# Turning the shifted bias tiles round: eight float32 matmuls with a flip matrix become 32 TensorE transposes with the same matrix

## What is computed

```python
def t5_bucket(dist):
    dist = jnp.maximum(dist, 0)
    ...
    return jnp.where(dist < BUCKET_MAX_EXACT, dist, large)
...
        bias = jnp.transpose(bias_tab[t5_bucket(dist)], (0, 3, 1, 2))
        logits = jnp.einsum('bqhd,bqkd->bhqk', qb, kg).astype(jnp.float32) * scale + bias.astype(jnp.float32)
```

## Time and profile before

| | us |
|---|---|
| median of 3 runs | 679.97 |
| lowest, highest | 677.24, 688.75 |
| the profiled execution | 680.09 |
| its span, first to last instruction | 678.3 |
| TensorE matmuls busy in the span | 614.6 |
| VectorE, ScalarE, GpSimd busy | 389.5, 309.0, 229.7 |

### The profile page before, as it was taken

The page is one execution under the profiler, slowest core; times in us unless marked ns, Lnnn a source line. Parts: engine busy times, 40 slices in busy tenths (PEclk is TensorE's granted clock), DMA queues, the critical chain, the costliest instruction groups (busy, mean ns, idle before and its releaser), DMA issues.

```text
span 678.3 us, 9664 instructions
## 1 busy us (share of the span) xinstructions
PE 614.6 (91%) x3658; PEld 389.0 (57%) x3658; DVE 389.5 (57%) x823; ACT 309.0 (46%) x502; POOL 229.7 (34%) x165
## 2 busy tenths in 40 slices
PE   1799999599899999789999999989999999799998
PEld 1344557365434866467767667755666677433443
DVE  6722394153579998986887866632325444567411
ACT  2555543223456685640431522354576676353610
POOL 1355540441203565440343341143632221143420
PEclk9999999699999999999999999998999999999999
DMA  8334533344101441320031021121121101252311
GB/s 279 93 103 138 166 104 92 125 125 124 48 1 50 124 125 31 94 60 4 1 93 32 1 63 32 32 63 32 31 63 63 63 32 32 62 187 93 133 57 59
DMA packets 31190, 52.78 MB, mean 78 GB/s; under 512 B 2759, under 2 KB 13345, under 8 KB 31145
## 3 DMA queue, kind: packets, MB, share of 16 engines
q1 hardware_dynamic: 29552, 51.19, 24.3%
q10 hardware_dynamic: 1593, 0.97, 0.5%
HBM read 50.04 MB, written 2.12 MB: 77 GB/s over the span
## 4 chain that ended last, share of the span: by engine, by line
PE 70%; DVE 16%; ACT 5%; issue 4%; POOL 3%; DMA 2%; DVEq 0%; SPq 0%; ACTq 0%; POOLq 0%
PE bank L1465 11%; PE bank L1467 11%; PE bank L1466 11%; PE bank L1651 8%; PE bank L1719 5%; PE bank L1721 5%; PE bank L1723 5%; PE bank L1827 3%; DVE work L1202 2%; PE bank L1539 2%; PE bank L1501 2%; PE bank L1846 2%; PE bank L1635 2%; POOL w_lo L466 2%; DVE early L1110 1%
## 5 line engine op out<-in xcount | busy, mean ns | idle before, releaser
L466 POOL TENSOR_TENSOR w_lo<-stage,w_hi 128x1024 f16<-128x1024 f32 (+5 forms) x80 | 157.1, 1971 | 236.5 <-ACT w_hi L699 236.3
L699 ACT ACTIVATE w_hi<-stage 128x1024 f16<-128x1024 f32 (+5 forms) x80 | 78.3, 979 | 22.4 <-PE bank L1467 12.6
L1651 PE MATMUL bank<-work 128*128 128x128 f32 x616 | 80.2, 279 | 8.7 <-DVEq L1177 8.5
L1651 PEld LDWEIGHTS bank<-work 128*128 128x128 f32 x616 | 75.9, 193 | 20.4 <-DVEq L1177 15.2
L694 ACT ACTIVATE stage<-stage 128x1024 f32<-128x1024 f32 (+5 forms) x80 | 77.5, 968 | 11.8 <-DMA stage<-in_w_in 11.4
L1719 PE MATMUL bank<-hT_hi,w_hi 128*128 128x512 f16 x192 | 74.3, 387 | 1.7 <-PE bank L1723 0.6
L1721 PE MATMUL bank<-hT_lo,w_hi 128*128 128x512 f16 x192 | 73.8, 385 | 0.4
L1723 PE MATMUL bank<-hT_hi,w_lo 128*128 128x512 f16 x192 | 73.8, 384 | 0.3
L1465 PE MATMUL bank<-w_hi,hT_hi 128*128 128x260 f16 (+4 forms) x192 | 63.1, 329 | 6.3 <-DVE hT_lo L929 3.0
L1466 PE MATMUL bank<-w_lo,hT_hi 128*128 128x260 f16 (+4 forms) x192 | 62.8, 327 | 0.0
L1467 PE MATMUL bank<-w_hi,hT_lo 128*128 128x260 f16 (+4 forms) x192 | 62.7, 326 | 0.0
(11 more groups left out here) (295 smaller groups left out, 1139.3 us busy)
## 6 DMA issues: line engine op xcount, KB each, us to landing
stage<-in_w_in SPq DMA_DIRECT2D x40, 512.0 KB, 3.6
stage<-in_c_phi_w SPq DMA_DIRECT2D x8, 512.0 KB, 3.9
stage<-in_w_branch SPq DMA_DIRECT2D x8, 512.0 KB, 3.7
stage<-in_w_out SPq DMA_DIRECT2D x8, 512.0 KB, 3.7
stage<-in_w_in SPq DMA_DIRECT2D x8, 260.0 KB, 2.8
strips<-rel_rows SPq DMA_DIRECT2D x8, 256.0 KB, 4.0
late<-in_x SPq DMA_DIRECT2D x1, 2048.0 KB, 9.0
out_x<-late SPq DMA_DIRECT2D x8, 256.0 KB, 2.0
```

What stands on the lines that cost most here:

```text
L466: gp.tensor_tensor(piece_view(w_lo[:, k % PAIRS, :], c), piece_view(stage[:, piece_at[c, j] % STAGES, :], c), piece_view(w_hi[:, k % PAIRS ...
L699: nc.scalar.activation(piece_view(w_hi[:, k % PAIRS, :], c), full, ACT.Copy).then_inc(hi_ready, 1)
L1651: ins = mm(ps[:, h * P:(h + 1) * P], lhs(h), rhs(h), start=True, stop=True)
```

## The change

The constant row runs from distance -127 upwards instead of from 511 downwards, so that `strips[p, j]` holds the distance p + j - 127. A transpose of the block of columns 128 n to 128 n + 127 with the flip matrix gives at (m, i) the entry (127 - i, 128 n + m), distance 128 n + m - i, and the four blocks are put down in reverse order. The tile that VectorE copies back is the same as before.

```diff
@@ -76,7 +76,7 @@
     f[:, F_FLIP:F_FLIP + P] = np.eye(P)[::-1]
     f[:, F_SEEN] = i >= CMP_BLOCK - 1
     f[:, F_SEEN + 1:F_SEEN + 4] = 1.0
-    dist = T - 1 - np.arange(S_REL)
+    dist = np.arange(S_REL) - (P - 1)
     ratio = np.log(np.maximum(dist, 1).astype(np.float32) / EXACT) / math.log(MAX_DIST / EXACT)
@@ -1584,7 +1584,9 @@
             def flips(*hs):
                 for h in hs:
                     ps = v_bank(("flip", h))
-                    mm(ps[:, :], flip, strips[:, h, :], start=True, stop=True).then_inc(v_filled, 1)
+                    for n in range(NT):
+                        ins = nc.tensor.transpose(ps[:, (NT - 1 - n) * P:(NT - n) * P], strips[:, h, n * P:(n + 1) * P], flip)
+                    ins.then_inc(v_filled, 1)
 
             def k_transposes(h):
                 transposes(("ak", h), columns(k_twice, P * h))
```

## The result

The changed kernel takes 684.79 us (684.05 to 685.95, 6 executions), the kernel before 680.17 us (677.24 to 688.75, 6 executions); the ratio is 1.0092 with a 95% interval of 1.0069 to 1.0114. Forecast were 677.0 us and a range up to 680.6. The kernel is slower by 0.9%, inside the 2% for which the forecast gave 0.97, but on the wrong side and outside the range.

A forecast was written before the change was run, and what follows sets the result against it. TensorE was taken as the bound, so its savings count in full: 2.62 us from six flips plus 0.45 from flip 7, 3.1 us, off 680.09 gives 677.0 us; range 674.2 to 680.6.

The forecast's parts named there:

- 0.44 and 0.47 us a head: B0 projection, flips 0 to 5: four transposes replace 0.86 or 0.94 us per head, so 2.62 us go.
- flip 6 worth nothing: End of B0: VectorE's two k_a operations hide flip 6, so its saving is 0 and TensorE waits about 0.4 us longer.
- (c): Behind 198 us VectorE sets the pace with work not waiting for TensorE, swallowing the saving; 680 us, chance 0.08.
- (d): At the flips, a mirrored identity makes each transpose run as a plain float32 matmul, 0.89 us; 680.3 us, chance 0.03.
- the 1.00 of the stretch from 152 to 182 us: Around the flips in B0: full clock was granted there, where four transposes held 0.44 us, answering the skill's rule.
- the last two flips: End of B0: flip 6 saves nothing, flip 7 is on the path and saves 0.45 us (0.42 to 0.68).
- (b): Clock falls at 178 us and stays down through the score stage, doubling 11.5 us of TensorE pieces; 688.5 us, chance 0.04.

The follow-up runs named there:

- e5: The changed kernel with eight float32 transposes into an unused PSUM bank in the wait before flip 7; 684.92 us.
- e4: The changed kernel with four half-precision products of 512 columns into an unused PSUM bank in the wait before flip 7; 680.95 us.
- e10: The changed kernel with the transposes of k for head 3 moved ahead of flip 5, so that flip 7 no longer waits; 674.92 us.
- e1: The changed kernel with flips 6 and 7 as plain float32 matmuls of the same operands; 685.97 us, and 684.52 us when run again.

## Why the prediction was wrong

**Right: the mechanism and size of the saving.** 0.44 and 0.47 us a head, flip 6 worth nothing, 3.1 us up to the first score, and 2.8 us between the lost groups of the two kernels. The rivals (c) and (d) are out. The rule that the full clock does not engage for transposes (the Trainium skill, "TensorE: Matmul & The Clock Gate", Part 4) had been answered with the 1.00 of the stretch from 152 to 182 us. That still stands among dense products. That eight transposes in the wait kept the clock in 3 of 10 executions against 0 of 32 without them (e5) fits the rule badly if it means that they count for nothing, though only one of the three is clear; no run here tells transposes from products with confidence.

**The step that failed** is the one on the last two flips, flip 6 above all: "its saving is worth nothing, and TensorE merely waits about 0.4 us longer than now". The wait came out as said, 1.19 us, but it wasn't free: with it, and the shorter flips beside it, all 16 executions lost the clock in a stage that could hold it only sometimes, in two of the three profiled ones at its entry, and the stage took 7.8 us longer. Work in the wait (e4, e5) or no wait (e10) brought kept executions back, 14 of 30 against 0 of 32. That it is the wait by itself, and not also the start time, is not shown: e1 with a wait of 0.74 us lost the clock in 13 of 14, though in its two profiles only 4 us into the scores. The price had been worked out, as rival (b): 688.5 us with a chance of 0.04; the profiled execution took 685.8. (b) doubled all 11.5 us; what came was 9.3 more on the 12 pieces (20.8 - 11.5), part of it in place of time in which ScalarE had held the chain, so that the stage grew by only 7.8.

**Why (b) got 0.04.** Its counter-argument was that the stage held 1.00 in the one profile there was. That was one execution of a kernel that loses the clock in 78 of 133; by that share the forecast of 677.0 us would have been a matter of luck even with the wait at no cost. The hint stood in the table of times: 688.75 us among 677.24 and 679.97, put down in the prediction to a median that may move by itself. It lay where (b) lay, 8.8 us above the median.

**What the change is worth.** It takes 2.8 us from the executions that had lost the clock anyway, 59 in 100, and adds 685.1 - 679.7 = 5.4 us to the other 41: -1.7 + 2.2 = +0.5 us. The means agree, 684.2 us for 133 executions of before, 684.8 for 16 of the changed kernel. The measured 0.9% compares with those that had kept the clock, and is their loss alone.

## What to carry to other kernels

Where TensorE waits for another engine anyway, a shorter instruction isn't free of consequences: ask what the added idle time does to the clock of the next stage, above all where that stage is itself full of short waits and can't win the clock back. Treat a single high time among few executions as a second behaviour of the kernel, look for the stage that has it, and count executions instead of comparing two medians. Cheap products into an unused bank in such waits were worth more here than the edit.

## What the runs showed of the hardware that I had not expected

One and the same program on one core gave two behaviours 8 us apart (medians 679.7 and 687.9), and as far as the profiles show the difference lies in one stage. A clock that had fallen there stayed at 1.2 GHz for 27 us (177.2 to 204.5 in the changed kernel), with TensorE busy for 13.95 of 15 us between 182 and 197, and came back only 2 us into a projection of half-precision products. In the kernel before the same stage was granted 1.00 with only 12.50 of 15 us busy: being busy in the records at half clock did not bring the clock back there, while the same score matmuls often kept it.
